# Feed-forward gate and up products with seven block products in place of eight

## The chip, the cores and the metric

The kernel runs on one core of a Trainium2 chip. The metric is the device time of one execution in microseconds; the time before is 2141.26 us, the median of three executions (2140.7 to 2142.35).

## The reference, cut to what matters

Two transformer blocks in float32 on 512 tokens of width 1024. The first block has two feed-forward layers; only their gate and up products change:

```python
D_FF = -(-8 * D_MODEL // (3 * 256)) * 256        # 2816

def swiglu(h, w_gu, w_down):
    u = h @ w_gu
    g, v = u[..., :D_FF], u[..., D_FF:]
    return (jax.nn.silu(g) * v) @ w_down

h = h + swiglu(rmsnorm(h, norm_g[layer, 1]), ffn_w_gu[layer], ffn_w_down[layer])
```

## The kernel before

Activations lie with features on the 128 partitions and the 512 tokens along the free axis, in KT = 8 chunks of features: `h[:, k, :]` is the residual, `hn_hi[:, k, :]` its product with the norm's gain, rounded to fp32r, and `hn_lo` the remainder. Each product runs as three fp32r matmuls in `three` (L652: high weight by high data, L653: by low data, L654: low weight by high data). The 1/rms per token (`rn`) is multiplied in after the product, on VectorE.

The 2816 columns of the gate and of the up half are 22 tiles of 128 each. A tile's weights come as one panel of 128x2048 floats (1 MB: 8 feature chunks of gate and up in turn) into `a_raw[v]`, v = tile mod 2, by a DMA on SP's queue (`load_a`). ScalarE copies the panel to fp32r (`high_a`, L1520), VectorE subtracts for the remainder (`low_a`, L2137). `linear` then makes the gate into PSUM bank 2v and the up half into bank 2v+1, 24 matmuls of 512 columns each. `load_b`, `high_b` (L1527) and `low_b` (L2143) do the same for the down weights, 128x1024. Per tile, VectorE scales the gate (L2407), ScalarE applies Silu (L1701), VectorE scales again (L2409) and multiplies by the up product (L2412, `hid`); ScalarE and VectorE split `hid` (L1703, L2414). `down` multiplies two tiles' `hid`, first that of the first tile (f = 0) into four banks, then that of the second (f = 1); it does so for two halves of the 1024 outputs, 48 matmuls of 512 columns per pair of tiles, and VectorE adds the eight results to `h` (`add_y`, L2236).

A feed-forward layer is 11 pairs of tiles. Each engine has its own program, run strictly in the order in which it is written, and they meet on counting semaphores; there is no scheduler. `a_ready` counts split panels: `load_a` may refill `a_raw[v]` once the tile in it is split. GpSimd has nothing to do in these stages beyond adding squares at their start (L3150).

## Time and profile before

| | us |
|---|---|
| median of three executions | 2141.26 |
| lowest, highest | 2140.7, 2142.35 |
| span of the profiled execution, first to last instruction | 2139.6 |
| first feed-forward layer, 246.28 to 606.10 | 359.82 |
| second feed-forward layer, 1036.50 to 1398.20 | 361.70 |

The profiled execution is known by its span, 1.7 us under the median of the executions that were timed. A window's start is the first matmul of the layer and its end the last of its `down`. Matmuls overlap in the records, so the distance from one start to the next is what one costs, not its duration.

### The profile page before, as it was taken

The numbers are of one execution on the slowest core, as the hardware profiler recorded it, in microseconds if no ns is written. First come the engines' busy times: TensorE is split into PE (matmuls) and PEld (weight loads), VectorE is DVE, ScalarE is ACT, GpSimd is POOL, SyncE is SP. The second block draws the span as 40 slices with busy tenths as digits, with TensorE's granted clock in tenths as the row PEclk, the third lists the DMA queues.
The fourth block names the chain that finished last, engine by engine and source line by source line (L and its number), as shares of the span: only waits on it lengthen the run. The fifth ranks groups of instructions, "written<-read, shape, count | busy, mean of one in ns | idle before, by whom it ended". The sixth has DMA issues, their size and how long they took to land.

```text
span 2139.6 us, 27223 instructions
## 1 busy us (share of the span) xinstructions
PE 2097.5 (98%) x10474; PEld 1579.8 (74%) x10474; DVE 1267.3 (59%) x1704; ACT 836.2 (39%) x1258; POOL 270.8 (13%) x234
## 2 busy tenths in 40 slices
...
GB/s 202 125 94 74 118 92 105 88 88 117 79 64 147 130 172 79 31 46 90 131 91 99 104 88 88 98 61 78 60 99 98 62 239 321 418 408 401 391 238 60
DMA packets 62622, 298.13 MB, mean 139 GB/s; under 512 B 14080, under 2 KB 14464, under 8 KB 34582
## 3 DMA queue, kind: packets, MB, share of 16 engines
...
q14 instruction: 31, 0.25, 0.0%
...
## 4 chain that ended last, share of the span: by engine, by line
PE 80%; DVE 8%; DMA 5%; ACT 3%; issue 2%; POOL 1%; POOLq 0%; ACTq 0%; DVEq 0%
PE psum L652 21%; PE psum L654 21%; PE psum L653 21%; PE psum L1413 5%; PE psum L1437 3%; DMA panel<-w_m 3%; PE psum L1102 2%; PE psum L1077 1%; DVE a_lo L2137 1%; DMA over_panel<-w_m,over_row 1%; ACT a_hi L1520 1%; DVE xc L2294 1%; DVE hs L2248 1%; ACT hn_hi L1547 0%; PE psum L1235 0%
## 5 line engine op out<-in xcount | busy, mean ns | idle before, releaser
L652 PE MATMUL psum<-hn_hi,a_hi 128*128 128x512 f32 (+1 forms) x1592 | 628.2, 395 | 1.9 <-DVE a_lo L2126 0.9
L654 PE MATMUL psum<-hn_hi,a_lo 128*128 128x512 f32 (+1 forms) x1592 | 618.5, 389 | 0.0
L653 PE MATMUL psum<-hn_lo,a_hi 128*128 128x512 f32 (+1 forms) x1592 | 618.1, 388 | 0.0
L652 PEld LDWEIGHTS psum<-hn_hi,a_hi 128*128 128x128 f32 (+1 forms) x1592 | 297.0, 187 | 73.5 <-issue 7.8
L653 PEld LDWEIGHTS psum<-hn_lo,a_hi 128*128 128x128 f32 (+1 forms) x1592 | 297.1, 187 | 64.8 <-issue 2.4
L654 PEld LDWEIGHTS psum<-hn_hi,a_lo 128*128 128x128 f32 (+1 forms) x1592 | 297.0, 187 | 64.4
L2137 DVE TENSOR_TENSOR a_lo<-a_raw,a_hi 128x2048 fp32r<-128x2048 f32 (+2 forms) x108 | 247.2, 2289 | 69.6 <-ACT a_hi L1520 69.1
L1520 ACT ACTIVATE a_hi<-a_raw 128x2048 fp32r<-128x2048 f32 (+2 forms) x108 | 201.3, 1866 | 71.2 <-PE psum L654 62.0
L2236 DVE TENSOR_TENSOR h<-h,psum 128x512 f32<-128x512 f32 x176 | 119.4, 686 | 78.4 <-PE psum L654 78.4
L3150 POOL TENSOR_TENSOR sq<-sq 128x512 f32<-128x512 f32 x5 | 7.8, 1555 | 1118.2 <-ACT sq L1533 1118.2
L3072 DVE TENSOR_TENSOR xhid<-xsg,psum 128x256 f32<-128x256 f32 x24 | 10.1, 421 | 232.3 <-ACT xsg L2081 232.3
L1701 ACT ACTIVATE sg<-sg 128x512 f32<-128x512 f32 x44 | 27.8, 632 | 286.2 <-DVE sg L2407 286.2
L652 PE MATMUL psum<-hid_hi,b_hi 128*128 128x512 f32 x352 | 137.3, 390 | 2.1 <-DVE h L2236 2.0
L654 PE MATMUL psum<-hid_hi,b_lo 128*128 128x512 f32 x352 | 137.0, 389 | 0.0
L653 PE MATMUL psum<-hid_lo,b_hi 128*128 128x512 f32 x352 | 136.9, 389 | 0.0
L1413 PE MATMUL psum<-panel,xw 128*64 128x512 f32 x512 | 113.4, 595 | 0.0
L2412 DVE TENSOR_TENSOR hid<-sg,psum 128x512 f32<-128x512 f32 x44 | 30.3, 688 | 113.8 <-PE psum L654 113.7
L1703 ACT ACTIVATE hid_hi<-hid 128x512 fp32r<-128x512 f32 x44 | 27.8, 632 | 177.5 <-DVE hid L2412 177.5
L1527 ACT ACTIVATE b_hi<-b_raw 128x1024 fp32r<-128x1024 f32 x64 | 66.9, 1050 | 65.5 <-PE psum L654 63.2
L1413 PEld LDWEIGHTS psum<-panel,xw 128*64 128x64 f32 x512 | 35.4, 137 | 66.8 <-issue 66.5
L2143 DVE TENSOR_TENSOR b_lo<-b_raw,b_hi 128x1024 fp32r<-128x1024 f32 x64 | 79.7, 1252 | 1.0 <-ACT b_hi L1527 1.0
L652 PEld LDWEIGHTS psum<-hid_hi,b_hi 128*128 128x128 f32 x352 | 66.1, 188 | 17.4 <-issue 2.6
...
## 6 DMA issues: line engine op xcount, KB each, us to landing
a_raw<-w_a SPq DMA_DIRECT2D x115, 1024.0 KB, 5.0
panel<-w_m SPq DMA_DIRECT2D x96, 1024.0 KB
b_raw<-w_b SPq DMA_DIRECT2D x64, 512.0 KB, 3.4
...
token_rows<-nat POOLq DMA_DIRECT2D x4, 512.0 KB, 5.5
```

The source lines that it names most:

```text
L652: pe.matmul(out, w_hi, x_hi, start=first, stop=False)
L653: pe.matmul(out, w_hi, x_lo, start=False, stop=False)
L654: return pe.matmul(out, w_lo, x_hi, start=False, stop=last)
L1102: mm = pe.matmul(bank[6 + at % 2][side * DV:(side + 1) * DV, t * P:(t + 1) * P], w, x, start=i == 0, stop=i == len(steps) - 1)
L1413: mm = pe.matmul(bank[v][rows, :], xw[:, v, k, rows], w[half][:, k % 4 * 2 * EFF:(k % 4 + 1) * 2 * EFF], start=k == 0, stop=k == KT - 1)
L1437: mm = pe.matmul(bank[4 + 2 * v + hb][rows, :], xturn[:, v, f * P + half * SLOTS:f * P + (half + 1) * SLOTS], w[half][:, f * D + hb * 512: ...
L1520: act.activation(a_hi[s % 2][:, 0:w], a_raw[s % 2][:, 0:w], ACT.Copy).then_inc(a_rounded, 1)
L1527: act.activation(b_hi[s % 2][:, :], b_raw[s % 2][:, :], ACT.Copy).then_inc(b_rounded, 1)
L2137: V.tensor_tensor(a_lo[s % 2][:, 0:w], a_raw[s % 2][:, 0:w], a_hi[s % 2][:, 0:w], ALU.subtract) \
L2143: V.tensor_tensor(b_lo[s % 2][:, :], b_raw[s % 2][:, :], b_hi[s % 2][:, :], ALU.subtract) \
L2236: V.tensor_tensor(h[:, m, :], h[:, m, :], bank[4 + m % 4][:, :], ALU.add).then_inc(y_free, 1)
L2412: V.tensor_tensor(hid[:, f, :], sg[:, f, :], ps[1][:, :], ALU.mult).then_inc(tile_free, 2)
```

## The change

Tiles 2 to 21 of each layer (20 of 22, ten pairs; tiles 0 and 1 stay as they were) are made from seven block products. A tile's panel is seen as a 2x2 block matrix (gate and up by feature chunks 0 to 3 and 4 to 7), and the tokens as two halves of 256. The four blocks are A_11, A_12 (gate), A_21, A_22 (up). The sums are S_1 = A_22 + A_21, S_3 = A_11 + A_21, S_2 = A_11 + S_1 and S_4 = A_12 + S_2. The data sums T1 to T4 of `tx` are made once per layer: eight scalings on ScalarE (`gain_x`), 16 additions and subtractions on GpSimd (`make_tx`), four splits each on ScalarE and VectorE.

A tile is then seven products (`seven`) of 12 matmuls of 256 columns, in this order in a phase of TensorE: P_1, P_2, then P_3 of the tile before, P_6, then P_4 of the tile before, P_7, P_5. `down` of a pair comes between the two phases of the next pair. P_6 and P_5 are added into the bank that P_1 left, after ScalarE has copied out what the bank held (`copy_1`, `copy_2`, `copy_3`). VectorE makes gate and up from the pieces by `add_11`, `scale_11`, `scale_12`, `add_21`, `add_22`.

The weight sums are made by DMAs that add, issued by GpSimd (`sum_panel`), 128x512 floats (256 KB) each: S_1 into `a_raw[v]`, S_3 and then S_2 into the tile `w_sum[:, v]`, S_4 into `a_raw[v]`. Two loads per tile, 256 KB each, put A_11 and A_21 into `w_sum` first. Split pieces stand in seven slots (`slot_hi`, `slot_lo`), single buffered. Panels are packed on the host as gate chunks, then up chunks. Several semaphores of earlier stages go on under new names (`w_used` is `gate_mm`, `w_rounded` is `m2_done`, `w_split` is `mult_done`, `part_copied` is `gelu_done`).

```diff
+            def load_fast(a, b, q):
+                sp.wait_ge(hn_ready, KT * (q + 1))
+                with sp.Fori(1, FF_TILES // 2) as i:
+                    for v in range(2):
+                        load_a(a + v, i)
+                        for x, c in ((S_2, 0), (S_3, 2 * S)):
+                            sp.dma_start(w_sum[:, v, x, :, :].rearrange("p k n -> p (k n)"),
+                                         w_a[ds(a + v + 2 * i, 1), :, c:c + S].rearrange("a p n -> p (a n)")) \
+                              .then_inc(sum_begun[v], 16)
+                        load_b(b + v, i)
...
-            def ffn(sa, sb_, e, trips, q, t):
-                linear_first(sa, q)
...
+            def seven(out, slot, x_hi, x_lo, again=False):
+                for k in range(KT // 2):
+                    mm = three(out, slot_hi[:, slot, k, :], slot_lo[:, slot, k, :], x_hi(k), x_lo(k),
+                               not again and k == 0, k == KT // 2 - 1, again)
+                return mm
...
+            def fast_phase(sa, g, i, v, between=None):
+                n, m = sa + v + 2 * i, v - 2 + 2 * i
+                first = isinstance(i, int) and m == 0
+                x, z, y = bank[2 * v][:, 0:HALF], bank[2 * v + 1][:, 0:HALF], bank[2 * v + 1][:, HALF:S]
+                split, copied = split_at(g) + 5 * m, copied_at(g) + 3 * m
+                pe.wait_ge(tile_free, 2 * n - 2)
+                pe.wait_ge(w_split, split + 1)
+                seven(x, P_1, *hn_block(0, slice(0, HALF))).then_inc(w_used, 1)
+                seven(y, P_2, *hn_block(KT // 2, slice(0, HALF))).then_inc(w_used, 1)
+                if not first:
+                    pe.wait_ge(part_copied, copied)
+                    pe.wait_ge(w_split, split + 2)
+                    seven(bank[2 - 2 * v][:, 0:HALF], P_3, *hn_block(KT // 2, slice(HALF, S)), again=True) \
+                        .then_inc(w_used, 1)
+                else:
+                    between()
+                    pe.wait_ge(tx_ready, tx_at(g + 1))
+                pe.wait_ge(part_copied, copied + 1)
+                pe.wait_ge(w_split, split + 4)
+                seven(x, P_6, *tx(T2), again=True).then_inc(w_used, 2 if first else 1)
+                if not first:
+                    pe.wait_ge(a_ready, n)
+                    pe.wait_ge(part_added, added_at(g) + 2 * m)
+                    seven(bank[3 - 2 * v][:, 0:HALF], P_4, *tx(T4), again=True).then_inc(tile_ready, 2)
+                pe.wait_ge(part_added, added_at(g) + 2 * m + 1)
+                seven(z, P_7, *tx(T3)).then_inc(w_used, 1)
+                pe.wait_ge(part_copied, copied + 2)
+                pe.wait_ge(w_split, split + 5)
+                seven(x, P_5, *tx(T1), again=True).then_inc(w_used, 1)
...
-                linear(sa + 1)
-                down(sb_, e, 0, hid_hi, hid_lo, P)
-                with pe.Fori(1, trips) as i:
-                    linear(sa, i)
-                    linear(sa + 1, i)
-                    down(sb_, e, i, hid_hi, hid_lo, P)
-            ffn(A_FF0, B_FF0, E_FF0, FF_TILES // 2, N_FFN0, T_FFN0)
+                linear(sa + 1, blocks=True)
+                fast_phase(sa, g, 1, 0, between=lambda: down(sb_, e, 0, hid_hi, hid_lo, P))
+                fast_phase(sa, g, 1, 1)
+                with pe.Fori(2, trips) as i:
+                    fast_phase(sa, g, i, 0)
+                    down(sb_ - 2, e - 1, i, hid_hi, hid_lo, P)
+                    fast_phase(sa, g, i, 1)
+                fast_last(sa, g)
+                down(sb_, e, trips - 1, hid_hi, hid_lo, P)
...
+            def high_s4(g, i, v):
+                act.wait_ge(w_summed[v], summed_at(g) + 64 * i)
+                act.wait_ge(w_used, used_at(g) + 6 * (v - 2 + 2 * i) + 3)
+                act.activation(slot_hi[:, P_3, :, :], part(v, S_4), ACT.Copy).then_inc(w_rounded, 1)
...
+            def high_s2(sa, g, i, v):
+                m = v - 2 + 2 * i
+                act.wait_ge(w_summed[v], summed_at(g) + 64 * i - 16)
+                if isinstance(i, int) and m == 0:
+                    act.wait_ge(tile_ready, 2 * sa + 2)
+                else:
+                    act.wait_ge(w_used, used_at(g) + 6 * (m - 1) + 4)
+                act.activation(slot_hi[:, P_6, :, :], w_sum[:, v, S_2, :, :], ACT.Copy).then_inc(w_rounded, 1)
...
+            def fast_a(sa, sb_, e, i, g):
+                copy_1(g, i, 0)
+                high_1(sa, g, i, 1)
+                high_s4(g, i, 0)
+                silu(e, i - 1, 1)
+                copy_2(sa, g, i, 0)
+                high_b(sb_ - 1, i)
+                high_a22(sa, i, 0)
+                high_hid(1, hid_made, hid_at(g) - 2 + 2 * i)
+                copy_3(g, i, 0)
+                high_s3(sa, g, i, 1)
+                high_s2(sa, g, i, 1)
+                high_s1(sa, g, i, 1)
+                high_b(sb_, i)
+            def fast_b(sa, e, i, g, last=False):
+                copy_1(g, i, 1)
+                if not last:
+                    high_1(sa, g, i + 1, 0)
+                high_s4(g, i, 1)
+                silu(e, i, 0)
+                copy_2(sa, g, i, 1)
+                high_a22(sa, i, 1)
+                high_hid(0, hid_made, hid_at(g) - 1 + 2 * i)
+                if not last:
+                    high_s3(sa, g, i + 1, 0)
+                    high_s2(sa, g, i + 1, 0)
+                copy_3(g, i, 1)
+                if not last:
+                    high_s1(sa, g, i + 1, 0)
...
+            def low_a22(n, v):
+                V.wait_ge(a_rounded, n + 1)
+                V.tensor_tensor(slot_lo[:, P_4, :, :], part(v, A_22), slot_hi[:, P_4, :, :], ALU.subtract).then_inc(a_ready, 1)
...
+            def add_21(n, v):
+                V.wait_ge(tile_ready, 2 * n + 2)
+                V.tensor_tensor(up[:, 0:HALF], bank[2 * v + 1][:, 0:HALF], pc2[:, v, :], ALU.subtract).then_inc(tile_free, 2)
+            def add_22(g, m, v):
+                V.wait_ge(part_copied, copied_at(g) + 3 * m + 3)
+                V.tensor_tensor(up[:, HALF:S], bank[2 * v + 1][:, 0:HALF], pc3[:, :], ALU.subtract).then_inc(part_added, 1)
...
+                low_b(sb_ + 1, trips - 1)
+                low_a(sa + FF_TILES)
+                scale_12(used_at(g + 1), 1)
+                scale_gate(e, trips - 1, 1)
+                add_21(sa + FF_TILES - 1, 1)
+                fast_hidden(e, sa + FF_TILES - 1, trips - 1, 1)
+                low_hid(e, trips - 1, 1)
...
+            def make_tx(g, k):
+                x = tx_of(k)
+                pool.wait_ge(x_gained, gained_at(g) + 2 * k + 2)
+                pool.tensor_tensor(x[:, 3, :], x[:, 1, :], x[:, 3, :], ALU.subtract).then_inc(tx_made, 1)
+                pool.tensor_tensor(x[:, 1, :], x[:, 0, :], x[:, 1, :], ALU.subtract).then_inc(tx_made, 1)
+                pool.wait_ge(tx_made, tx_at(g, 4) + 4 * k + 1)
+                pool.tensor_tensor(x[:, 0, :], x[:, 3, :], x[:, 0, :], ALU.subtract).then_inc(tx_made, 1)
+                pool.wait_ge(tx_made, tx_at(g, 4) + 4 * k + 3)
+                pool.tensor_tensor(x[:, 2, :], x[:, 2, :], x[:, 0, :], ALU.add).then_inc(tx_made, 1)
+            def sum_panel(sa, g, i, v):
+                done = summed_at(g) + 64 * i
+                pool.wait_ge(a_loaded[(sa + v) % 2], 16 * ((sa + v) // 2 + i) + 16)
+                pool.wait_ge(sum_begun[v], begun_at(g) + 32 * i)
+                pool.dma_start(part(v, S_1), part(v, A_22), accum_op=ALU.add).then_inc(w_summed[v], 16)
+                pool.dma_start(w_sum[:, v, S_3, :, :], part(v, A_11), accum_op=ALU.add).then_inc(w_summed[v], 16)
+                pool.wait_ge(w_summed[v], done - 32)
+                pool.dma_start(w_sum[:, v, S_2, :, :], part(v, S_1), accum_op=ALU.add).then_inc(w_summed[v], 16)
+                pool.wait_ge(w_summed[v], done - 16)
+                pool.wait_ge(w_split, split_at(g) + 5 * (v - 2 + 2 * i) + 1)
+                pool.dma_start(part(v, S_4), w_sum[:, v, S_2, :, :], accum_op=ALU.add).then_inc(w_summed[v], 16)
+            def ffn(sa, g):
+                for k in range(KT // 2):
+                    make_tx(g, k)
+                for i in range(1, FF_TILES // 2):
+                    for v in range(2):
+                        sum_panel(sa, g, i, v)
...
-        return _cols(w, [[slice(f * P, (f + 1) * P), slice(n + f * P, n + (f + 1) * P)] for f in range(n // P)])
+        panels = _cols(w, [[slice(f * P, (f + 1) * P), slice(n + f * P, n + (f + 1) * P)] for f in range(n // P)])
+        return panels.reshape(-1, P, KT, 2, P).transpose(0, 1, 3, 2, 4).reshape(-1, P, WA)```

ScalarE in the loop over pairs, for the second tile of a pair. Before, `a_hi` and `b_hi` are the splits of the two panels; after, `slot_hi` are the splits of blocks and sums (from `w_sum` first S_3, then S_2), and `pc` the copies of partial products.

```order
L1520 ACTIVATE a_hi<-a_raw 128x2048 [waits tile_ready]
L1526 ISA [waits b_loaded1_then_w_ple_loaded]
L1527 ACTIVATE b_hi<-b_raw 128x1024 [waits y_ready]
L1700 REGISTER_ALU
L1701 ACTIVATE sg<-sg 128x512 [waits gate_scaled]
L1702 REGISTER_ALU
L1703 ACTIVATE hid_hi<-hid 128x512 [waits tile_free]
```

```order
L1841 ACTIVATE hid_hi<-hid 128x512 [waits scan_done_then_hid_made]
L1864 ISA
L1868 REGISTER_ALU [waits w_summed0_then_y_stored0]
L1869 ACTIVATE slot_hi<-w_sum 128x512 [waits gate_mm_then_w_used]
L1873 REGISTER_ALU
L1877 REGISTER_ALU [waits w_summed0_then_y_stored0]
L1878 ACTIVATE slot_hi<-w_sum 128x512 [waits gate_mm_then_w_used]
L1903 REGISTER_ALU
L1905 REGISTER_ALU [waits gate_mm_then_w_used]
L1906 ACTIVATE pc<-psum 128x256 [waits xc_done_then_part_added]
```

The copy of a tile's last partial product (L1906) now stands behind the splits of the next tile's S_3 and S_2 (L1869, L1878), which wait for the adding DMAs.

GpSimd after the data sums of the first layer, one tile of each buffer; `a_raw` and `w_sum` as above.

```order
L3592 DMA a_raw<-a_raw 128x512 [waits xb_taken_then_sum_begun0,a_loaded0]
L3593 DMA w_sum<-a_raw 128x512
L3595 DMA w_sum<-a_raw 128x512 [waits w_summed0_then_y_stored0]
L3598 DMA a_raw<-w_sum 128x512 [waits mult_done_then_w_split,w_summed0_then_y_stored0]
L3592 DMA a_raw<-a_raw 128x512 [waits gel_scaled_then_sum_begun1,a_loaded1]
```

Where GpSimd issued nothing before, it now issues four adding DMAs per tile, the third behind the landing of the first two and the fourth behind that of the third, and the next tile's behind all of them.

VectorE at the end of the first layer, before and after, down to the last split of `hid`. `a_lo` is the split of the next stage's first panel, `up` the up product.

```order
L2137 TENSOR_TENSOR a_lo<-a_raw,a_hi 128x2048 [waits a_rounded]
L2143 TENSOR_TENSOR b_lo<-b_raw,b_hi 128x1024 [waits b_rounded]
L2407 TENSOR_TENSOR sg<-psum,rn 128x512 [waits tile_free,tile_ready]
L2409 TENSOR_TENSOR sg<-sg,rn 128x512 [waits gate_done]
L2412 TENSOR_TENSOR hid<-sg,psum 128x512 [waits tile_ready,gate_scaled]
```

```order
L2730 TENSOR_TENSOR up<-psum,pc 128x256 [waits gelu_done_then_part_copied]
L2415 TENSOR_TENSOR b_lo<-b_raw,b_hi 128x1024 [waits b_rounded]
L2409 TENSOR_TENSOR a_lo<-a_raw,a_hi 128x1536 [waits a_rounded]
L2722 TENSOR_TENSOR sg<-psum,rn 128x256 [waits gate_mm_then_w_used]
L2734 TENSOR_TENSOR sg<-sg,rn 128x512 [waits gate_done]
L2726 TENSOR_TENSOR up<-psum,pc 128x256 [waits tile_ready]
L2739 TENSOR_TENSOR hid<-sg,up 128x512 [waits tile_free,gate_scaled]
L2682 TENSOR_TENSOR hid_lo<-hid,hid_hi 128x512 [waits hid_rounded]
```

The split of the next panel stood ahead of the last gate's scaling before too, when TensorE had the whole up half of that tile still to do. Now it stands behind an `up` piece that waits for the last tile's P_5, when only P_3 and P_4 are left.

## Rows read from the trace of the kernel before

**Rows 1.** The page: its first line and TensorE's share of the span.
```profile
span 2139.6 us, 27223 instructions
...
PE 2097.5 (98%) x10474; PEld 1579.8 (74%) x10474; DVE 1267.3 (59%) x1704; ACT 836.2 (39%) x1258; POOL 270.8 (13%) x234
```

**Rows 2.** Windows over the two feed-forward blocks: start:end, us, busy of each engine.
```profile
246.28:606.10 359.82, 358.80 (x1580) 296.22 (x1579) 202.08 (x229) 98.33 (x102) 1.11 (x2) 1.00 0.25 93
1036.50:1398.20 361.70, 360.57 (x1588) 297.71 (x1587) 205.99 (x234) 100.89 (x105) 2.77 (x5) 1.00 0.26 96
```

**Rows 3.** Waits of TensorE, first block, then second: total, times, longest.
```profile
PE psum L652 <- DVE h L2236: 0.9, 1, 0.9
PE psum L652 <- DVE h L2236: 1.1, 2, 0.9
```

**Rows 4.** Timeline, 512-column matmuls and a weight load: start, duration, engine.
```profile
300.04 0.39 PE L652 MATMUL psum<-hn_hi,a_hi 128*128 128x512 f32 x1
300.27 0.39 PE L653 MATMUL psum<-hn_lo,a_hi 128*128 128x512 f32 x1
300.27 0.19 PEld L654 LDWEIGHTS psum<-hn_hi,a_lo 128*128 128x128 f32 x1
```

**Rows 5.** Timeline of 256-column matmuls (three), then their weight loads grouped.
```profile
704.02 0.28 PE L654 MATMUL psum<-a_hi,hn_lo 128*128 128x256 f32 x1
704.14 0.28 PE L652 MATMUL psum<-a_hi,hn_hi 128*128 128x256 f32 x1
704.26 0.28 PE L653 MATMUL psum<-a_lo,hn_hi 128*128 128x256 f32 x1
L653 PEld LDWEIGHTS psum<-a_lo,hn_hi 128*128 128x128 f32 x55 | 10.6, 192 | 0.0
```

**Rows 6.** Groups of VectorE, 300 to 596 us: count, busy, mean ns.
```profile
L2236 DVE TENSOR_TENSOR h<-h,psum 128x512 f32<-128x512 f32 x72 | 49.1, 687 | 35.7 <-PE psum L654 35.7
L2137 DVE TENSOR_TENSOR a_lo<-a_raw,a_hi 128x2048 fp32r<-128x2048 f32 x18 | 41.2, 2289 | 10.0 <-ACT a_hi L1520 10.0
L2143 DVE TENSOR_TENSOR b_lo<-b_raw,b_hi 128x1024 fp32r<-128x1024 f32 x18 | 21.9, 1218 | 0.0
...
L2414 DVE TENSOR_TENSOR hid_lo<-hid,hid_hi 128x512 fp32r<-128x512 f32 x18 | 12.5, 692 | 12.6 <-ACT hid_hi L1703 12.6
...
L2407 DVE TENSOR_TENSOR sg<-psum,rn 128x512 f32<-128x512 f32 x18 | 12.4, 687 | 13.4 <-PE psum L654 13.4
```

**Rows 7.** Groups of ScalarE, 300 to 596 us.
```profile
L1520 ACT ACTIVATE a_hi<-a_raw 128x2048 fp32r<-128x2048 f32 x18 | 34.2, 1901 | 0.0
L1527 ACT ACTIVATE b_hi<-b_raw 128x1024 fp32r<-128x1024 f32 x18 | 18.9, 1051 | 19.9 <-PE psum L654 19.9
L1701 ACT ACTIVATE sg<-sg 128x512 f32<-128x512 f32 x19 | 12.0, 632 | 127.1 <-DVE sg L2407 127.1
```

**Rows 8.** Groups elsewhere with 256 elements: VectorE, then ScalarE.
```profile
L3072 DVE TENSOR_TENSOR xhid<-xsg,psum 128x256 f32<-128x256 f32 x24 | 10.1, 421 | 232.3 <-ACT xsg L2081 232.3
L2081 ACT ACTIVATE xsg<-psum 128x256 f32<-128x256 f32 x24 | 9.2, 384 | 139.6 <-PE psum L1413 133.4 <-issue 6.1
```

**Rows 9.** The 1536-element splits, 590 to 640 us: VectorE, then ScalarE.
```profile
L2137 DVE TENSOR_TENSOR a_lo<-a_raw,a_hi 128x1536 fp32r<-128x1536 f32 x1 | 1.8, 1751 | 0.0
L1520 ACT ACTIVATE a_hi<-a_raw 128x1536 fp32r<-128x1536 f32 x1 | 1.5, 1475 | 0.0
```

**Rows 10.** DMA issues: count, KB of one, median us to landing.
```profile
a_raw<-w_a SPq DMA_DIRECT2D x115, 1024.0 KB, 5.0
...
b_raw<-w_b SPq DMA_DIRECT2D x64, 512.0 KB, 3.4
...
dk<-decay POOLq DMA_DIRECT2D x1, 1024.0 KB, 5.2
...
ptr<-p_t POOLq DMA_DIRECT2D x1, 512.0 KB, 6.9
...
cs<-rope POOLq DMA_DIRECT2D x1, 256.0 KB, 3.1
```

**Rows 11.** GpSimd: a 512-element addition's group and a DMA issue's.
```profile
L3150 POOL TENSOR_TENSOR sq<-sq 128x512 f32<-128x512 f32 x5 | 7.8, 1555 | 1118.2 <-ACT sq L1533 1118.2
L3203 POOL DMA_DIRECT2D q_scratch<-q_hi x7 | 4.7, 677 | 31.8 <-DVE qb_lo L2568 31.8
```

416 lines of the change are left out of this document (333 added, 83 removed).

## The prediction

> **What bounds the kernel now.** The page comes first: TensorE is busy 98% of the span [rows 1]. A busy share alone does not make it the bound, so next the windows over the two feed-forward layers: 358.80 of 359.82 us and 360.57 of 361.70 us busy, at a granted clock of 1.00, with VectorE at 202 to 206 us, ScalarE near 100 and the DMA engines at a quarter [rows 2]. Then who makes TensorE wait: only VectorE's additions to `h`, 0.9 and 1.1 us in all [rows 3]. So TensorE ends last throughout both layers, and the time there is the number of matmuls by their spacing. The rest of the kernel is not touched.
>
> **What is removed.** A layer has 22x48 + 11x48 = 1584 wide matmuls; 358.80/1584 gives 0.2265 us each, as the starts 0.23 us apart in the timeline show [rows 2, 4]. A tile's gate and up cost 48x0.2265 = 10.87 us.
>
> **What stands in their place.** 7x12 = 84 matmuls of 256 columns. The change has fewer columns by an eighth, but 36 more instructions and weight loads per tile. The nearest row is a stage in which the same helper runs 128x128 weights by 256 columns in the same type: the starts are 0.12 us apart, each with a load whose record is 192 ns long, and these overlap without a gap [rows 5]. That is more than half of 0.2265 (0.113), so a fixed 0.013 us per matmul is paid more often. A tile then costs 84x0.120 = 10.08 us. Saved: 0.79 us by 40 tiles = 31.6 us. The bounds: 0.113 would save 55 us; 0.125 saves 15. I take 0.120, since operands, sizes and type agree.
>
> The TensorE page of the Trainium skill (TensorE: Matmul & The Clock Gate), section LDWEIGHTS and the mechanism under Packing small matmuls, says that a load takes columns/1.2 ns, 107 ns for 128, and overlaps a running matmul only in another row group. By that rule a load and a 256-column matmul would follow each other, and the change would lose far more than it saves; the spacing of 0.12 us with a load in each disagrees.
>
> **The other engines, per tile.** VectorE before: 2.29 (a_lo) + 1.22 (b_lo) + 4x0.69 + 4x0.69 (`add_y`) = 9.0 us. After: two of 1024 elements at 1.22, eight of 512 at 0.69 (five remainders, gate, `hid`, its remainder), four `add_y` at 0.69, five of 256 at 0.42: 12.8 us [rows 6, 8]. A tile's share of a pair is 10.08 + 5.44 = 15.5 us of TensorE, so VectorE goes from 55% to 83%. ScalarE: two of 1024 at 1.05, seven of 512 at 0.63, three copies of 256 at 0.38 = 7.7 us, half of the time [rows 7, 8]. Both fit; what counts is where they stand in their programs. The chain from a tile's last product P_4 to its split `hid` is add_21 0.42, hid 0.69, 0.63 and 0.69 plus one 1024-element split in between, 3.7 us; it is needed only for f = 1 of `down`, behind P_7, P_5 (24x0.12 = 2.9 us) and twelve wide matmuls (2.7 us). Inside a phase every copy (0.38 us) has at least one product of 1.44 us behind it. I cost all this at nothing, with 0.8 us in all for small waits. If this cover were gone, each 0.4 us per phase would cost 16 us.
>
> The 1.0 us per layer that TensorE waits for `h` goes too, as `down` comes later against the additions: 2.0 us [rows 3].
>
> **The adding DMAs.** The trace has none, neither SBUF to SBUF nor adding, and their time L from issue to landing decides. A plain 256 KB load on GpSimd's queue lands in 3.1 us, one of 1024 KB in 5.2, one of 512 KB beside indirect ones in 6.9 [rows 10]. An adding DMA reads source and destination, 512 KB; between 3.1 and 5.2 that is 3.8 us. Bounds: 3.1 and 6.9; I take 3.8, since no indirect DMA runs beside it. GpSimd takes 0.68 us to issue one [rows 11]. The loads: 1 MB lands in 5.0 us, 512 KB in 3.4, so 1.5 MB (panel and the two blocks for `w_sum`) in 6.6 [rows 10].
>
> From the panel's refill the chain is: 0.7 to the load's issue, 6.6 to land, 0.7 issue, 1.2 for the second adder beside the first, L; then 0.7 + L (S_2); then 0.7 + L (S_4).
>
> In the loop, with time 0 at the start of `down`: `a_raw[0]` is free at 1.1, loaded at 8.4, S_2 landed at 10.9 + 2L, S_4 at 11.6 + 3L. S_2 must be split before ScalarE comes to `copy_3`, on which P_3 of the next phase waits: at 10.9 (`down`) + 10.1 (phase) + 2.9 (P_1, P_2) - 0.9 = 23.0, which allows L up to 6.0. S_4 stands ahead of `copy_2`, on which P_5 waits: due at 28.1, L up to 5.5. And GpSimd's order: the other buffer's panel is there at 26.7, its S_2 at 29.2 + 2L, and only then may the next tile's adders go, due at 31.0 + 8.4, L up to 5.1. So with 3.8 the loop has room, and from about 5.2 on it does not.
>
> **Where it does not fit.** At the start of a layer, phases one and two of the new kind follow each other without `down` between. S_2 of the third new tile takes 0.7 + 6.6 + 0.7 + 1.2 + 3.8 + 0.7 + 3.8 + 0.5 (split) + 0.4 (`copy_3`) = 18.4 us from the refill; TensorE has 0.8 + 10.1 + 2.9, about 14.0 us of work. Wait: 4.4 us per layer, 8.8 us. The start itself, with eight scalings more on ScalarE (5.0 us) and 16 GpSimd additions of half the 1.56 us row (12.5 us) [rows 7, 11], is hidden: `tx` is needed only after 48 wide matmuls of tile 1, P_1, P_2 and all of `down`, 24.6 us.
>
> At a layer's end, behind P_5: copy_3 0.38, b_hi 1.05, the next stage's a_hi 1.48 (1.90 in the second layer) and a_lo 1.75 (2.29) [rows 7, 9], then scale_12 0.42, Silu 0.63, gate 0.69, add_21 0.42, hid 0.69, 0.63, 0.69: 8.8 and 9.8 us. TensorE has P_3 and P_4 (2.9) and f = 0 of `down` (2.7). Wait: 3.2 and 4.2 us, 7.4 us in all, of which some 0.6 at P_3, for copy_3.
>
> **The sum:** -31.6 - 2.0 + 8.8 + 7.4 + 0.8 = -16.6 us. 2139.6 - 16.6 = 2123.0 us of span; the median of the timed executions lies 1.7 us above the profiled span, so 2124.7, say 2125 us.
>
> The DMA page of the Trainium skill (DMA: Bandwidth & Descriptors), section Anatomy of one DMA, fits a GpSimd-issued DMA at 2.0 us + bytes/436e3. As an estimate from it, 512 KB would take 3.2 us; the sum would then be 2.4 us lower, since only the two starts hang on it. The plain row of 3.1 us for 256 KB is above the page's 2.6, and the row is what I go by.
>
> **The rivals.**
> A. The adding DMAs are slow, L above 5.2 (slower). For: 512 KB took 6.9 us once, four adders per tile share the engines with 2 MB of loads, and they depend on each other three deep; ScalarE's and GpSimd's strict order turns one late sum into late copies. Against: the DMA engines are a quarter busy [rows 2]. Price: beyond 5.2 each us costs 2 to 3 us per pair, some 50 us over 20 pairs. The 16 us are gone at L = 5.5; L = 6.0 gives about 2165, 6.9 about 2210. Chance 0.22.
> B. The strict order costs more than I see: 0.3 to 0.5 us per phase, because VectorE at 83% is late with a remainder or a sum. 40 phases: 12 to 20 us back, 2135 to 2145. Against: the longest stretch of VectorE between two things that TensorE waits for is shorter than its cover wherever I followed it. Chance 0.12.
> C. Loads are not hidden behind narrow matmuls: 84 times at least 0.19 against 48x0.2265, 5 us more per tile, about 2340. It is the skill's rule above; rows 5 speak against it. Chance 0.02.
> D. It goes better: L at 3.1 and the waits at start and end half as long, 2117. Chance 0.06.
> The forecast, 2119 to 2133: 0.58.
>
> **How the numbers follow.** A change within 0.2% (4.3 us) can't be told from none. Faster: forecast, D, a third of B: 0.68. Same: half of B and the edge of A: 0.09. Slower: most of A, C, and the rest: 0.23. The range goes from 2117 (D) to 2158, which takes in B and the first half of A; the slower half of A and C stay out.
>
> **What would show it.** In the loop: starts of the slot matmuls 0.120 us apart; a pair 31.0 us against 32.6; no waits of TensorE but one near 4.4 us at the first P_3 of the loop, on ScalarE's copy, and one near 3 to 4 us in the last `down`, on `hid`. The adding DMAs landing within 5 us. The prediction is wrong if TensorE waits in each pair for ScalarE's copies while ScalarE waits for `w_sum` (A), if it waits for VectorE (B), or if the spacing is not 0.120 (C).

## The result and the profile after

The changed kernel takes 2193.83 us (median of four executions, 2188.91 to 2202.2) against 2141.03 for the one before: a ratio of 1.0251, 95% interval 1.0229 to 1.0272. Predicted were 2125 us and a range up to 2158.

The page, which answers to [rows 1]:

```profile
span 2192.7 us, 32213 instructions
...
PE 2089.8 (95%) x11914; PEld 1636.4 (75%) x11914; DVE 1399.3 (64%) x2072; ACT 968.6 (44%) x1602; POOL 443.4 (20%) x426
```

The windows over the first layer, over a stretch of its loop and over the second layer (columns as in [rows 2]; the last three are the granted clock, the DMA engines' busy share and GB/s):

```profile
246.28:628.95 382.67, 356.29 (x2305) 326.24 (x2304) 269.80 (x415) 166.25 (x276) 89.66 (x99) 0.98 0.68 173
315.00:600.00 285.00, 267.17 (x1785) 247.13 (x1784) 194.66 (x313) 112.60 (x194) 56.11 (x65) 0.99 0.73 183
1059.50:1451.40 391.90, 357.05 (x2299) 325.97 (x2298) 270.38 (x416) 167.77 (x278) 89.27 (x100) 0.97 0.68 172
```

The whole loss lies in the two layers: 382.67 us in place of 359.82, and 391.90 in place of 361.70 [rows 2]. TensorE is idle there for some 60 us, and the DMA share, 0.25 and 0.26 before [rows 2], is 0.68 over a layer and 0.73 in the loop.

Who makes TensorE wait, over the whole span (us, times, longest):

```profile
PE psum L735 <- ACT pc L1899: 44.3, 26, 2.7
PE psum L735 <- ACT pc L1906: 8.6, 6, 3.4
PE psum L735 <- DVE hid_lo L2682: 6.3, 2, 3.8
```

And ScalarE, in the first layer:

```profile
ACT slot_hi L1878 <- DMA w_sum<-a_raw: 89.1, 19, 9.5
ACT slot_hi L1849 <- DMA a_raw<-w_a: 28.0, 8, 3.8
...
ACT slot_hi L1855 <- DMA a_raw<-w_sum: 21.8, 12, 4.0
```

The second and third rows of TensorE are the two waits that the prediction counted (8.8 and 7.4 us), though not all of the second row stands where it had put it (see below). The first is new: `copy_2` (L1899) is late, because ScalarE has stood before the splits of S_2 (L1878), of the next panel (L1849) and of S_4 (L1855), all waiting for DMAs. In the first layer VectorE is not named but for `hid_lo`. That is the picture of rival A.

The timeline shows why. First the third adder (S_2) with nothing beside it, then the same step 18 us later, with SyncE's refill of the other buffer issued 0.4 us before it (start, duration, engine; in brackets the idle time before and its releaser):

```profile
400.35 0.86 POOL L3595 DMA_DIRECT2D w_sum<-a_raw  x1 [3.38 <-DMA w_sum<-a_raw]
403.79 0.33 SPq L609 DMA_DIRECT2D a_raw<-w_a  x1
403.89 0.86 POOL L3598 DMA_DIRECT2D a_raw<-w_sum  x1 [2.69 <-DMA w_sum<-a_raw]
...
412.07 0.63 ACT L1855 ACTIVATE slot_hi<-a_raw 128x512 fp32r<-128x512 f32 x1 [1.21 <-DMA a_raw<-w_sum]
...
412.93 0.86 POOL L3592 DMA_DIRECT2D a_raw<-a_raw  x1 [8.18 <-DMA w_sum<-w_a]
413.47 1.21 POOL L3593 DMA_DIRECT2D w_sum<-a_raw  x1
...
417.68 0.33 SPq L609 DMA_DIRECT2D a_raw<-w_a  x1
418.05 0.86 POOL L3595 DMA_DIRECT2D w_sum<-a_raw  x1 [3.38 <-DMA w_sum<-a_raw]
418.11 0.91 SPq L635 DMA_DIRECT2D w_sum<-w_a  x2
...
427.25 0.63 ACT L1878 ACTIVATE slot_hi<-w_sum 128x512 fp32r<-128x512 f32 x1 [8.75 <-DMA w_sum<-a_raw]
427.51 0.86 POOL L3598 DMA_DIRECT2D a_raw<-w_sum  x1 [8.60 <-DMA w_sum<-a_raw]
```

Alone, S_2 lands within 3.5 us (400.35 to 403.89, where GpSimd issues the DMA that waits for it); S_1 and S_3 together take 5.1 (412.93 to 418.05). Beside a refill, S_4 takes 8.2 (403.89 to 412.07) and S_2 9.2 (418.05 to 427.25). The refill suffers too: `a_raw<-w_a` takes a median of 7.1 us in the loop in place of 5.4, the loads into `w_sum` 7.4.

What an adding DMA costs the DMA engines can be read from its queue in the stretch 315 to 600 us (queue: packets, MB, share of 16 engines). q0 holds GpSimd's DMAs, 65 of them here, q1 SyncE's loads:

```profile
q1 hardware_dynamic: 9504, 35.13, 38.4%
q0 software_dynamic: 9379, 17.05, 34.6%
```

0.346 x 285/65 = 1.52 us of all 16 engines each, as an estimate from these rows. A plain load costs 0.384 x 285/35.13 = 3.1 us per MB, 0.82 us for the same 256 KB.

### The profile page after: what moved, and what is told of

It is laid out like the page before. It is cut to its first block, busy times and chain, and to the rows that moved or that the text cites. A ratio compares the mean times of both kernels' runs of the same rounds, so it can differ in the third digit from the quotient of the medians.

```text
span 2192.7 us, 32213 instructions
## 1 busy us (share of the span) xinstructions
PE 2089.8 (95%) x11914; PEld 1636.4 (75%) x11914; DVE 1399.3 (64%) x2072; ACT 968.6 (44%) x1602; POOL 443.4 (20%) x426
## 3 DMA queue, kind: packets, MB, share of 16 engines
q8 instruction: 68, 1.11, 0.2%
## 4 chain that ended last, share of the span: by engine, by line
PE 54%; DMA 19%; DVE 11%; issue 8%; ACT 5%; POOL 3%; SPq 1%; DVEq 0%; ACTq 0%; POOLq 0%
PE psum L735 13%; PE psum L736 13%; PE psum L737 12%; DMA w_sum<-a_raw 6%; DMA w_sum<-w_a 4%; PE psum L1550 4%; DMA panel<-w_m 4%; PE psum L1574 3%; DMA a_raw<-w_sum 2%; PE psum L1239 2%; PE psum L1214 1%; DVE h L2508 1%; DVE a_lo L2409 1%; POOL w_sum L3593 1%; POOL a_raw L3592 1%
## 5 line engine op out<-in xcount | busy, mean ns | idle before, releaser
L735 PE MATMUL psum<-hn_hi,a_hi 128*128 128x512 f32 (+2 forms) x952 | 379.1, 398 | 1.9 <-DVE a_lo L2398 0.9
L737 PE MATMUL psum<-hn_hi,a_lo 128*128 128x512 f32 (+2 forms) x952 | 369.5, 388 | 0.0
L736 PE MATMUL psum<-hn_lo,a_hi 128*128 128x512 f32 (+2 forms) x952 | 369.2, 388 | 0.0
L735 PE MATMUL psum<-tx_hi,slot_hi 128*128 128x256 f32 x640 | 187.7, 293 | 44.5 <-ACT pc L1899 44.3
L735 PEld LDWEIGHTS psum<-hn_hi,a_hi 128*128 128x128 f32 (+1 forms) x952 | 176.8, 186 | 48.9 <-issue 8.2
L736 PEld LDWEIGHTS psum<-hn_lo,a_hi 128*128 128x128 f32 (+1 forms) x952 | 177.0, 186 | 39.9 <-issue 2.7
L737 PEld LDWEIGHTS psum<-hn_hi,a_lo 128*128 128x128 f32 (+1 forms) x952 | 176.8, 186 | 39.3
L2409 DVE TENSOR_TENSOR a_lo<-a_raw,a_hi 128x2048 fp32r<-128x2048 f32 (+3 forms) x68 | 155.7, 2290 | 46.8 <-ACT a_hi L1657 46.2
L737 PE MATMUL psum<-tx_hi,slot_lo 128*128 128x256 f32 x640 | 184.3, 288 | 0.0
L736 PE MATMUL psum<-tx_lo,slot_hi 128*128 128x256 f32 x640 | 184.3, 288 | 0.0
L735 PEld LDWEIGHTS psum<-tx_hi,slot_hi 128*128 128x128 f32 x640 | 125.5, 196 | 50.7 <-DVE slot_lo L2692 46.6
L3479 DVE TENSOR_TENSOR xhid<-xsg,psum 128x256 f32<-128x256 f32 x24 | 10.1, 421 | 231.9 <-ACT xsg L2353 231.9
L735 PE MATMUL psum<-hid_hi,b_hi 128*128 128x512 f32 x352 | 141.4, 402 | 6.8 <-DVE hid_lo L2682 6.3
L735 PE MATMUL psum<-hn_hi,slot_hi 128*128 128x256 f32 x480 | 137.1, 286 | 10.0 <-ACT pc L1906 8.6
L736 PE MATMUL psum<-hid_lo,b_hi 128*128 128x512 f32 x352 | 140.8, 400 | 0.0
L737 PE MATMUL psum<-hid_hi,b_lo 128*128 128x512 f32 x352 | 139.7, 397 | 0.0
L737 PE MATMUL psum<-hn_hi,slot_lo 128*128 128x256 f32 x480 | 136.6, 285 | 0.0
L736 PE MATMUL psum<-hn_lo,slot_hi 128*128 128x256 f32 x480 | 136.5, 284 | 0.0
L737 PEld LDWEIGHTS psum<-tx_hi,slot_lo 128*128 128x128 f32 x640 | 126.1, 197 | 0.0
L736 PEld LDWEIGHTS psum<-tx_lo,slot_hi 128*128 128x128 f32 x640 | 126.0, 197 | 0.1
## 6 DMA issues: line engine op xcount, KB each, us to landing
a_raw<-w_a SPq DMA_DIRECT2D x115, 1024.0 KB, 5.4
panel<-w_m SPq DMA_DIRECT2D x96, 1024.0 KB
b_raw<-w_b SPq DMA_DIRECT2D x64, 512.0 KB, 3.5
w_sum<-w_a SPq DMA_DIRECT2D x80, 256.0 KB, 7.3
w_sum<-a_raw POOLq DMA_DIRECT2D x80, 256.0 KB
a_raw<-a_raw POOLq DMA_DIRECT2D x40, 256.0 KB
a_raw<-w_sum POOLq DMA_DIRECT2D x40, 256.0 KB
```

Of the source, the lines that this page charges most:

```text
L735: pe.matmul(out, w_hi, x_hi, start=first, stop=False, skip_group_check=again)
L736: pe.matmul(out, w_hi, x_lo, start=False, stop=False, skip_group_check=again)
L737: return pe.matmul(out, w_lo, x_hi, start=False, stop=last, skip_group_check=again)
L2409: V.tensor_tensor(a_lo[s % 2][:, 0:w], a_raw[s % 2][:, 0:w], a_hi[s % 2][:, 0:w], ALU.subtract) \
```

## The experiments

All times are medians; the ratio is to the kernel before, with its 95% interval.

**Is it the adding DMAs?** Two runs take something from them, one takes from the loads beside them, and one changes the order on the engines that wait for them.

e1_tiny_adds: the four adding DMAs move 128x16 elements in place of 128x512 (the weight sums are left out, all waits stay). One of the four lines:

```diff
-pool.dma_start(part(v, S_1), part(v, A_22), accum_op=ALU.add)
+pool.dma_start(part(v, S_1)[:, 0:1, 0:16], part(v, A_22)[:, 0:1, 0:16], accum_op=ALU.add)
```

> The four adding DMAs of a tile are cut to 128x16 floats each (8 KB); the rest of each weight sum is left out, all waits and issues stay. If the adding DMAs' own data are what is late (they share the DMA engines with 1.5 MB of loads), nearly all waits on ScalarE's copies go, the granted clock no longer falls, and the time is that of the sum made before: about 2125 us. If instead issue and chaining through GpSimd cost the time, or the order on VectorE does, it stays above 2160 us.

e2_plain_copies: the same four DMAs of 256 KB, copying in place of adding (the sums are left out). One of the four lines:

```diff
-pool.dma_start(part(v, S_1), part(v, A_22), accum_op=ALU.add)
+pool.dma_start(part(v, S_1), part(v, A_22))
```

> The same four DMAs of 256 KB without the addition: plain copies inside SBUF, so the sums are left out and the blocks are copied. If the addition (a second read per byte) is what loads the DMA engines, the S_2 landing beside a refill falls from 9 to about 6 us and the time to 2130 to 2150 us. If any SBUF-to-SBUF transfer of this size collides with the refill, it stays near 2190 us.

e3_small_loads: from the second new pair on, the two loads into `w_sum` move 128x16 elements (S_2 and S_3 then start from old data).

> The two extra loads of 256 KB per tile into w_sum are cut to 128x16 floats from the second pair on (the sums then start from stale values); the adding DMAs stay whole. If the collision with the refill is the cause, its length counts: 1.0 instead of 1.5 MB beside the adding DMA takes some 2.5 us off each late S_2 and lets the adders start 2 us earlier, and most waits go: 2130 to 2150 us. If the adding DMAs are slow by themselves, little changes: above 2175 us.

e4_order: everything is computed; ScalarE and VectorE do the copies, Silu and `hid` ahead of the splits that wait for DMAs, in both phases. ScalarE's part for the second phase:

```diff
 copy_1(g, i, 1)
+silu(e, i, 0)
+copy_2(sa, g, i, 1)
 if not last:
     high_1(sa, g, i + 1, 0)
+high_hid(0, hid_made, hid_at(g) - 1 + 2 * i)
 high_s4(g, i, 1)
-silu(e, i, 0)
-copy_2(sa, g, i, 1)
 high_a22(sa, i, 1)
-high_hid(0, hid_made, hid_at(g) - 1 + 2 * i)
+copy_3(g, i, 1)
...
```

> Nothing is left out. ScalarE copies the partial products (copy_2, copy_3) and does Silu before it waits for the DMA-fed splits (high_1, high_s4, high_s3, high_s2), and VectorE likewise. If the strict order turns late sums into late copies, the waits on copy_2 go (S_4 is due only after the next product or down) and those on copy_3 shrink: 2135 to 2165 us. If the sums are late for TensorE itself, the waits move to the slots with the same length: 2185 us or more.

Measured: e1_tiny_adds 2131.18 us (0.9954, 0.9938 to 0.9971); e2_plain_copies 2131.29 (0.995, 0.9933 to 0.9966); e3_small_loads 2147.33 (1.0033, 1.0015 to 1.005); e4_order 2178.18 (1.0179, 1.0162 to 1.0196). Without the adders' bytes, or without the addition in them, the loss is gone: copies of the same bytes cost as little as tiny DMAs. But it is not the adders by themselves. With all four kept whole and only the two loads beside them cut, all but 6 us of the loss is gone too. It takes both.

With the order changed, 16 us of 53 come back. That lies between the two expectations (2135 to 2165, or 2185 and more): in the first layer the waits on `copy_2` go and those on `copy_3` shrink to 0.9 us, but TensorE now waits 11.3 us for `h` and 8.0 us for `copy_1`.

The queue's rows of e2_plain_copies, 64 DMAs in the same stretch, beside those above:

```profile
q1 hardware_dynamic: 9792, 37.23, 38.1%
q0 software_dynamic: 5120, 16.78, 15.4%
```

0.154 x 285/64 = 0.69 us each: the addition more than doubles what the DMA engines spend on the same bytes, with 144 packets in place of 80.

What the addition does to the time goes through the question which DMA meets a refill. The loop's start in e1_tiny_adds, where S_2 is an adder of 8 KB:

```profile
297.37 0.86 POOL L3595 DMA_DIRECT2D w_sum<-a_raw  x1 [1.43 <-DMA w_sum<-a_raw]
...
297.51 0.33 SPq L609 DMA_DIRECT2D a_raw<-w_a  x1
...
302.59 0.63 ACT L1878 ACTIVATE slot_hi<-w_sum 128x512 fp32r<-128x512 f32 x1 [4.66 <-DMA w_sum<-a_raw]
```

Issued 0.14 us before a refill, even these 8 KB take 5.2 us. So most of the time beside a refill is not spent on the adder's own bytes. The times at which the semaphores `w_summed` rise in the traces give every landing from 315 to 600 us. In the changed kernel S_2 of one buffer takes 8.5 to 9.9 us (once 5.5) and of the other 3.3; S_4 of that other buffer takes 7.9 to 8.2. In e1_tiny_adds S_2 always lands in 2.0 us in that stretch, ahead of the refill. Only one buffer's S_4 meets the refill, 6.1 to 7.7 us for 8 KB, and TensorE does not wait for it there; e2_plain_copies is alike (2.3, and 6.3 to 6.8). An adder is slower than a copy even when alone (3.3 us against 2.3), and three of them hang on each other, so that S_2 of one buffer comes to stand beside a refill.

**Do the adders and the refill only meet at a bad moment, or are the DMA engines too full?** d1_late_refill holds SyncE's loads back until S_2 of the tile before has landed.

```diff
+sp.wait_ge(w_summed[1 - v], summed_at(g) + 64 * i + 64 * v - 80)
 load_a(a + v, i)
```

> The kernel after, with SyncE's loads for a tile held back until S_2 of the tile before has landed; nothing else is changed. If it is the meeting of S_2 with the refill that costs (S_2 3.5 us alone, 9.2 beside the refill), ScalarE's wait for S_2 (89 us in the first layer) falls by more than half, the panel comes some 3 us later but loads in 7 to 9 us in place of 11, and the time is 2150 to 2185. If the DMA engines are simply too full (share 0.73), the wait only moves from S_2 to the panel and S_4, and the time is 2190 to 2230.

2245.45 us (1.0481, 1.0464 to 1.0499), worse than either theory had it. ScalarE's wait for S_2 in the stretch 315 to 600 us fell as the first theory says; the first row is of the changed kernel, the second of this run:

```profile
ACT slot_hi L1878 <- DMA w_sum<-a_raw: 67.5, 15, 9.3
```

```profile
ACT slot_hi L1886 <- DMA w_sum<-a_raw: 37.5, 15, 3.3
ACT slot_hi L1857 <- DMA a_raw<-w_a: 35.4, 8, 4.6
```

S_2 no longer meets a refill at all: 3.3 to 3.7 us by the rises of its semaphore. But refill and S_4 now start together every time, S_4 takes 8.3 to 9.1 us, and the wait for the panel grows from 28.0 to 35.4 us: each wait put ahead of a load makes the next panel and the next sums later. So both theories hold in part, and neither had the size. Part of the extra loss is the clock: TensorE's granted clock is 0.94 there, against 0.99.

**How much adding is too much, and what makes the sums better?** e5_two_adds makes S_1 and S_3 plain copies (these sums are left out) and lets S_2 and S_4 add.

> The kernel after, with two of a tile's four adding DMAs (S_1 and S_3) as plain copies of the same size; S_2 and S_4 still add. The sums S_1 and S_3 are left out. With no DMA adding 2131.3, with four 2193.8. If the cost is a limit that is run into (landing over about 5.2 us beside the refill, as the prediction had it for single DMAs), two adding DMAs with a DMA share of about 0.64 give 2131 to 2150. If each adding DMA costs its share, the time is the middle, 2155 to 2170.

g1_gpsimd and g2_gpsimd_order make the sums by GpSimd's additions, g3_one_dma all but S_4, which stays an adding DMA; none has loads into `w_sum`, and everything is computed. g2_gpsimd_order also has the order of e4_order. Two of the four sums in g1_gpsimd:

```diff
-pool.dma_start(part(v, S_1), part(v, A_22), accum_op=ALU.add).then_inc(w_summed[v], 16)
-pool.dma_start(w_sum[:, v, S_3, :, :], part(v, A_11), accum_op=ALU.add).then_inc(w_summed[v], 16)
+pool.tensor_tensor(w_sum[:, v, S_3, :, :], part(v, S_1), part(v, A_11), ALU.add).then_inc(w_summed[v], 16)
+pool.tensor_tensor(part(v, S_1), part(v, S_1), part(v, A_22), ALU.add).then_inc(w_summed[v], 16)
```

> The four weight sums of a tile are made by four additions on GpSimd in place of four adding DMAs, and the two loads into w_sum are gone; everything is computed. Theory 1 (the adding DMAs and what they do to the loads beside them were the whole loss, and a sum that is there in time costs nothing): GpSimd needs four times 1.5 to 2.2 us (its rows with 512 elements) = 6.0 to 8.8 us of a tile's 15.5, S_2 is there some 5 to 6 us after the panel in place of 8.4, and the time is that of the run with tiny adding DMAs, 2131, 2128 to 2134. DMA share in the loop falls from 0.73 to about 0.28. Theory 2 (GpSimd's and VectorE's additions get in each other's way; VectorE is busy 0.77 of the loop): VectorE's 512-element subtraction rises above its 0.69 us, TensorE waits on VectorE, and the time is 2145 or more. Theory 3 (what was lost has to do with the order of the engines, not with the DMAs): no nearer to before than 2165.

> The same, with ScalarE's and VectorE's order of the run e4_order (copies, Silu and hid ahead of the splits). If the sums come in time the order gains nothing: 2128 to 2140, and the wait of copy_1 and of the down product on h that the new order brought there (11.3 and 8.0 us in a layer) goes with the late sums. If those waits belong to the order itself, they stay, and the time is 20 to 40 us above that of g1_gpsimd.

> Three sums on GpSimd, S_4 alone still by an adding DMA, no loads into w_sum. The load on the DMA engines of adding DMAs falls to a quarter, and the one that is left runs beside the refill. Theory 1: S_4 beside a 1 MB refill lands in 4 to 6 us (5.2 to 5.4 in the run with small loads), which its place in the order allows (5.5), so the time is within 5 us of g1_gpsimd. A theory by which each adding DMA beside a refill costs, whatever their number: S_4 lands in 8 us, copy_2 is late, and the time is over 2150.

Measured: e5_two_adds 2142.11 us (1.0002, 0.9992 to 1.0011); g1_gpsimd 2165.11 (1.0108, 1.0091 to 1.0125); g2_gpsimd_order 2201.91 (1.0275, 1.0257 to 1.0292); g3_one_dma 2147.07 (1.0025, 1.0015 to 1.0035). Theory 1 fell for GpSimd, theory 2 holds: the DMA share is back to 0.27, and VectorE becomes the late one. (2165 is also the bound of theory 3, the order of the engines; e1_tiny_adds with the same order and 2131 speaks against it.) An addition of each beside the other in g1_gpsimd, and a subtraction of the same size a little later with GpSimd idle:

```profile
399.99 1.29 POOL L3593 TENSOR_TENSOR a_raw<-a_raw,w_sum 128x512 f32<-128x512 f32 x1 [2.37 <-DVE slot_lo L2682]
400.07 1.76 DVE L2688 TENSOR_TENSOR slot_lo<-a_raw,slot_hi 128x512 fp32r<-128x512 f32 x1
...
403.48 0.68 DVE L2692 TENSOR_TENSOR slot_lo<-a_raw,slot_hi 128x512 fp32r<-128x512 f32 x1
```

1.76 us in place of 0.68, though GpSimd's addition takes only 1.29. The Trainium skill (SBUF — State Buffer, Who interferes with whom) says that a VectorE instruction with two inputs in SBUF contends with a GpSimd instruction that reads SBUF; the rows agree. VectorE's busy time in 315 to 600 us is 236.75 us, 19 more than in e1_tiny_adds (217.54), and TensorE waits for the split of `hid` (12.1 us in the first layer). g2_gpsimd_order lies 37 us above g1_gpsimd. My expectation had 20 to 40 for the case that the waits of e4_order stay, but they did not: TensorE waits 27.8 us of the first layer for the split of `hid`, whose median there is 1.22 us in place of 0.69. g3_one_dma was to be within 5 us of g1_gpsimd; it is 18 us faster, with one addition less on GpSimd. Its S_4 lands in 3.3 to 3.5 us.

**Both costs in part.** g4_two_two makes S_3 and S_2 (as S_3 + A_22) on GpSimd, S_1 and S_4 by adding DMAs, and has no loads into `w_sum` (in the cut the waits between the four are left out). g5_two_two_end also puts the split of the next stage's panel behind that of the last `hid`, on ScalarE and VectorE.

```diff
+pool.tensor_tensor(w_sum[:, v, S_3, :, :], part(v, S_1), part(v, A_11), ALU.add)
+pool.dma_start(part(v, S_1), part(v, A_22), accum_op=ALU.add)
+pool.tensor_tensor(w_sum[:, v, S_2, :, :], w_sum[:, v, S_3, :, :], part(v, A_22), ALU.add)
+pool.dma_start(part(v, S_4), w_sum[:, v, S_2, :, :], accum_op=ALU.add)
...
-low_a(sa + FF_TILES)
 scale_12(used_at(g + 1), 1)
...
 low_hid(e, trips - 1, 1)
+low_a(sa + FF_TILES)
```

> Two sums of a tile on GpSimd (S_3, and S_2 as S_3 + A_22), two by adding DMAs (S_1, S_4), no loads into w_sum; everything is computed. By the account of the runs so far an adding DMA costs all 16 DMA engines 1.5 us, and an addition on GpSimd stretches one of VectorE by about 0.6 us. DMA share in the loop 0.28 + 2 x 1.5/15.5 = 0.47, VectorE's busy share some 0.02 below the 0.81 of g3_one_dma. If both costs matter only where they run into a limit, the time lies between the 2131 of the runs without the additions and the 2147 of g3_one_dma: 2133 to 2142. If adding DMAs cost by their number, it is 2147 plus a third of what lies between 2131 and 2194: 2160 or more.

> The same, with the split of the next stage's panel put behind that of the last hid of a layer, on ScalarE and on VectorE (this undoes the order at the layer's end for which the prediction counted 7.4 us). If that split is what TensorE waits for at the end, its wait on hid_lo (2.5 us in the first layer) goes in both layers and the time is 4 to 7 us under that of g4_two_two. If the wait is the chain of the last tile itself (scale, add, multiply, split), nothing changes.

Measured: g4_two_two 2136.59 us (0.9982, 0.9973 to 0.9991); g5_two_two_end 2134.69 (0.9968, 0.9956 to 0.998). Both beat the kernel before, by 4 and by 6 us. The longest wait on `hid_lo` at the end of the first layer went from 2.5 to 1.4 us there. The 1.9 us between the two are less than expected (4 to 7), and their intervals overlap.

The window 315 to 600 us of these runs, one by one. Read the busy time of PE (second number) and of DVE (fourth), then clock and DMA share ahead of the GB/s. The kernel before:

```profile
315.00:600.00 285.00, 285.00 (x1259) 236.08 (x1258) 152.99 (x172) 71.95 (x72) 0.00 (x0) 1.00 0.26 96
```

e1_tiny_adds:

```profile
315.00:600.00 285.00, 282.04 (x1919) 262.69 (x1918) 217.54 (x342) 128.93 (x215) 56.62 (x66) 0.99 0.42 131
```

e2_plain_copies:

```profile
315.00:600.00 285.00, 282.05 (x1919) 262.68 (x1918) 217.96 (x344) 128.69 (x216) 34.24 (x64) 0.99 0.54 190
```

e3_small_loads:

```profile
315.00:600.00 285.00, 280.26 (x1908) 260.73 (x1907) 214.38 (x340) 125.57 (x212) 56.13 (x65) 0.99 0.65 162
```

e5_two_adds:

```profile
315.00:600.00 285.00, 279.33 (x1911) 259.91 (x1911) 214.57 (x339) 125.20 (x211) 46.51 (x65) 1.00 0.64 191
```

e4_order:

```profile
315.00:600.00 285.00, 273.39 (x1854) 252.23 (x1854) 202.21 (x328) 116.59 (x205) 57.17 (x66) 0.99 0.73 184
```

d1_late_refill:

```profile
315.00:600.00 285.00, 261.20 (x1678) 241.07 (x1678) 189.23 (x297) 110.10 (x185) 53.56 (x62) 0.94 0.70 175
```

g1_gpsimd:

```profile
315.00:600.00 285.00, 274.52 (x1875) 253.67 (x1876) 236.75 (x334) 121.12 (x210) 98.32 (x67) 1.00 0.27 94
```

g3_one_dma:

```profile
315.00:600.00 285.00, 280.90 (x1908) 259.70 (x1908) 231.36 (x342) 124.49 (x213) 89.56 (x67) 0.99 0.37 115
```

g4_two_two:

```profile
315.00:600.00 285.00, 281.97 (x1925) 262.44 (x1924) 228.07 (x346) 127.83 (x217) 70.62 (x65) 1.00 0.47 132
```

Up to a DMA share of 0.54 the time is that of tiny DMAs, at 0.64 it is 2142, at 0.73 2194: a limit that is run into, not a price per DMA. The share is a warning and not the cause, though: e4_order has the same 0.73 with 2178, and d1_late_refill 0.70 with 2245. Nearer to the cause is the slower S_2 of a pair: 2.0 us in e1_tiny_adds, 2.3 in e2_plain_copies, 3.5 to 5.8 in e5_two_adds, 6.4 to 7.3 in the loop of e4_order and 8.5 to 9.9 in the changed kernel, with d1_late_refill (3.3 to 3.7) as the one that pays in the panel in its stead. With GpSimd's additions VectorE's busy time is the number to watch (228 us: 2137, 231: 2147, 237: 2165).

## Why the prediction was wrong

**What is removed and what stands in its place: right.** The slot matmuls start 0.120 us apart, as forecast from the helper's other stage. The timeline of e1_tiny_adds in the first layer, in which the first row also ends the wait at the layer's start (next point):

```profile
303.63 0.38 PE L735 MATMUL psum<-hn_hi,slot_hi 128*128 128x256 f32 x1 [3.73 <-ACT pc L1906]
303.85 0.28 PE L736 MATMUL psum<-hn_lo,slot_hi 128*128 128x256 f32 x1
303.97 0.28 PE L737 MATMUL psum<-hn_hi,slot_lo 128*128 128x256 f32 x1
...
305.52 0.41 PE L735 MATMUL psum<-tx_hi,slot_hi 128*128 128x256 f32 x1
305.73 0.41 PE L736 MATMUL psum<-tx_lo,slot_hi 128*128 128x256 f32 x1
305.95 0.41 PE L737 MATMUL psum<-tx_hi,slot_lo 128*128 128x256 f32 x1
```

That settles rival C as well: there are as many weight loads as matmuls (1918 and 1919 in the window of e1_tiny_adds above), so a load is hidden behind each. The sentence of the Trainium skill (TensorE: Matmul & The Clock Gate, the mechanism under Packing small matmuls) by which a load overlaps only in another row group does not describe them; the same section also names a background weight buffer for loads that run ahead, which the prediction did not weigh.

**The start of a layer: right in sum, in part by luck.** Predicted 4.4 us per layer at the first P_3 of the loop on `copy_3`; all waits on L1906 in the changed kernel are 8.6 us against 8.8. The chain was right for the changed kernel's first layer: 18.3 us from the refill (issued at 286.49) to the end of `copy_3` (304.75), predicted 18.4. The place was not:

```profile
291.76 0.38 PE L735 MATMUL psum<-hn_hi,slot_hi 128*128 128x256 f32 x1 [2.12 <-ACT pc L1906]
...
304.89 0.38 PE L735 MATMUL psum<-hn_hi,slot_hi 128*128 128x256 f32 x1 [1.30 <-ACT pc L1906]
```

TensorE waits 2.12 us one phase earlier, for S_2 of the second new tile, which meets that refill (5.0 us), and so only 1.30 at the predicted place. The 3.73 us with tiny adders have the predicted place, but another make: the first two sums land sooner than forecast there, and S_2 takes 5.2 us beside the refill.

**The end of a layer: right.** Predicted 3.2 and 4.2 us, of which some 0.6 in the two at P_3. Measured 2.5 and 3.8 on `hid`, and 0.75 and 0.47 at P_3: 3.2 and 4.3.

**The failed step is under "The adding DMAs": "their time L from issue to landing decides ... I take 3.8, since no indirect DMA runs beside it", and "So with 3.8 the loop has room".** For an adder alone 3.8 was good: 3.5 measured, and 5.1 for the first pair where 1.2 + 3.8 = 5.0 were counted. But L is no constant. The schedule that I wrote down has S_4 of the first buffer and S_2 of the second in flight while the other buffer's refill runs, and there L is 8 to 9 us, far beyond the 5.2 at which, by the same schedule, the loop no longer fits. The rule was right, the number that went in was for an idle queue. Nor was the reason in the adder's own bytes, by which the prediction put 3.8 between 3.1 and 5.2: 8 KB beside a refill take 5.2 to 7.7 us.

I could have seen it from rows 2. I weighed rival A down with "the DMA engines are a quarter busy", a share of before, and never added what the change puts on them. A plain load costs 0.258 x 285/27.27 = 2.7 us of 16 engines per MB in the loop before (its queue row below), so 0.71 us for 256 KB. Four adders as two accesses each are 8 x 0.71, the two loads 2 x 0.71, together 7.1 us in a tile's 15.5: as an estimate, 0.46 on top of 0.26 makes 0.72. Measured: 0.73. So close a match is partly luck, since the prices came out higher (1.52 us for an adder, 0.82 for a load) and the tiles took longer. And the share tells that landings will stretch, not by how much or which.

```profile
q1 hardware_dynamic: 4896, 27.27, 25.8%
```

**The sum against the measurement**, from the distances between starts of matmuls in both layers of the changed kernel, which run a little above the idle times in the rows, since the records overlap. TensorE's waits are 29.2 and 38.5 us, 67.7 in all, where 17 were predicted (8.8 + 7.4 + 0.8): +50.7. Matmuls spaced wider than at full clock without a wait are 10.4 and 11.6: +22.0, predicted none. The span came out 2192.7 - 2123.0 = 69.7 us over the forecast. The two make 72.7, 3 us too many. These are not outside the layers, where both kernels take 1418.1 us; a part is matmuls whose record is missing (2299 in the second window, where a layer has 2304), which this count takes for wide spacing, and the rest is not resolved.

**The clock was missing from the sum.** The rows of e1_tiny_adds from 305.52 on are 0.21 us apart in place of 0.12: half clock, 2 us after a wait of 3.7. The windows of e1_tiny_adds around the two long waits of the first layer, the only ones of that layer with a clock below 1.00:

```profile
302.00:306.00 4.00, 2.37 (x15) 2.37 (x16) 2.71 (x6) 2.88 (x6) 2.47 (x3) 0.84 0.43 121
306.00:310.00 4.00, 4.00 (x27) 4.00 (x27) 2.62 (x5) 2.61 (x5) 1.14 (x3) 0.74 0.13 4
590.00:594.00 4.00, 3.13 (x9) 2.49 (x10) 2.00 (x4) 2.30 (x4) 0.00 (x0) 0.68 0.21 90
594.00:598.00 4.00, 4.00 (x17) 3.26 (x16) 3.87 (x7) 2.80 (x5) 0.00 (x0) 0.90 0.00 0
```

0.16 + 0.26 of 4 us is 1.7 us of work lost after the first wait, 0.32 + 0.10 the same after the second. Four such waits in two layers make 6.7 us, about the difference between the 2131 of e1_tiny_adds and the forecast of 2125. In sum the forecast without slow adders was thus right but for this term. A wait of that length need not bring it: in g5_two_two_end TensorE waits 2.6 us for `h` in the first layer and its clock is 1.00 throughout, while behind the same wait of 2.6 us in g4_two_two it is 0.69 and 0.88 in the two windows of 4 us from 280 us on.

**The rivals.** A happened. Its price was stated for one L (50 us per us beyond 5.2, 2210 at 6.9), and there is no one L: of S_2 and S_4 in a pair two land in 3.3 us and two in 8 to 10, and the time is 2194. B did not: in the changed kernel and in e1_tiny_adds, with VectorE at 217.54 of 285 us, VectorE is named in TensorE's waits of the first layer for the last `hid` alone. It becomes real with GpSimd's additions: a little in g4_two_two, with VectorE at 228 us (3.9 us on `hid_lo`, 2.6 on `h` in the first layer), and clearly in g1_gpsimd at 237 (12.1 on `hid_lo`).

What stays open: how much of the 44.3 us on `copy_2` hangs on S_2, on S_4 and on the late panel. The three waits follow each other on ScalarE, and no run separates them. It is also open why a DMA of 8 KB waits so long beside a refill; no run splits the refill into smaller DMAs or puts it on another queue.
